# Three of the four branch products of the first two layers computed as split products, their weights parted in place by ScalarE and VectorE

## What is computed

```
gates = sigmoid(h @ w_in[:, gate columns])          # 256 x (4 * 1024)
merged = sum over b of gates[b] * (y[b] @ w_branch[b])   # y[b]: 256 x 256, w_branch[b]: 256 x 1024
x = x + merged @ w_out
```

## Time and profile before

| | |
|---|---|
| median of three runs | 2550.53 us (2550.09 to 2550.73) |
| the profiled execution, its own time | 2556.48 us |
| its span | 2554.7 us |
| PE busy, share of the span | 95% |
| DVE, ACT, POOL busy, share of the span | 67%, 54%, 16% |
| mean granted clock of PE | 0.972 |

### The profile page before, as it was taken

One profiled execution on the slowest core, in us unless ns is written; L12 is line 12 of the kernel. 1 busy time (PEld: TensorE's weight loads), 2 busy tenths in 40 slices (PEclk: granted clock), 3 DMA queues, 4 the chain that ended last, 5 costly groups with the idle time before them and its releaser, 6 DMA issues.

```text
span 2554.7 us, 31962 instructions
## 1 busy us (share of the span) xinstructions
PE 2414.3 (95%) x11845; PEld 1962.0 (77%) x11845; DVE 1708.3 (67%) x2332; ACT 1376.3 (54%) x1737; POOL 409.3 (16%) x225
## 2 busy tenths in 40 slices
PE   6999999899987999999999999899989989998998
PEld 6986788798766778778787787677768867776886
DVE  4848655566675889889889898863565555356554
ACT  4543344454422778778778787635334444533443
POOL 2155000003530000000000000065500006560000
PEclk9999999999997999999999999999999999999999
DMA  7434465244232999999999999653465525346550
GB/s 224 165 116 169 168 223 198 91 151 163 102 131 95 365 338 350 346 331 364 330 330 365 328 345 351 223 170 132 149 229 191 198 76 172 132 149 222 190 198 34
DMA packets 381700, 549.38 MB, mean 215 GB/s; under 512 B 27220, under 2 KB 283592, under 8 KB 381464
## 3 DMA queue, kind: packets, MB, share of 16 engines
q1 hardware_dynamic: 377392, 535.82, 61.5%
q0 software_dynamic: 3920, 11.58, 1.7%
q10 hardware_dynamic: 288, 0.59, 0.1%
HBM read 546.91 MB, written 1.05 MB: 214 GB/s over the span
## 4 chain that ended last, share of the span: by engine, by line
PE 83%; DVE 11%; DMA 3%; ACT 2%; issue 1%; POOL 0%; DVEq 0%; SPq 0%; ACTq 0%
PE mb L907 14%; PE mb L909 14%; PE mb L908 14%; PE pb L907 8%; PE pb L909 8%; PE pb L908 8%; DMA ring<-in_w_in 3%; PE pb L1356 2%; PE mb L1266 1%; PE pb L1027 1%; PE pb L1306 1%; DVE w_lo L2553 1%; PE pb L890 1%; PE mb L1054 1%; PE mb L1282 1%
## 5 line engine op out<-in xcount | busy, mean ns | idle before, releaser
L2553 DVE TENSOR_TENSOR w_lo<-ring,w_hi 128x1024 fp32r<-128x1024 f32 x444 | 533.5, 1222 | 193.4 <-ACT w_hi L1652 168.7
L1652 ACT ACTIVATE w_hi<-ring 128x1024 fp32r<-128x1024 f32 x340 | 348.2, 1054 | 310.9 <-PE pb L909 119.1
L907 PE MATMUL mb<-w_hi,hT_hi 128*128 128x512 f32 x1232 | 494.1, 401 | 3.0 <-DVE w_lo L2553 2.6
L909 PE MATMUL mb<-w_lo,hT_hi 128*128 128x512 f32 x1232 | 481.5, 391 | 0.0
L759 POOL TENSOR_TENSOR w_lo<-ring,w_hi 128x1024 fp32r<-128x1024 f32 x152 | 372.4, 2477 | 448.6 <-ACT w_hi L1652 448.5
L907 PE MATMUL pb<-w_hi,hT_hi 128*128 128x512 f32 (+1 forms) x928 | 355.7, 383 | 19.3 <-DVE low_rows L2553 6.8
L2553 DVE TENSOR_TENSOR w_lo<-down_w,w_hi 128x1024 fp32r<-128x1024 f32 x242 | 293.9, 1223 | 88.2 <-ACT w_hi L1652 79.5
L909 PE MATMUL pb<-w_lo,hT_hi 128*128 128x512 f32 (+1 forms) x928 | 346.3, 373 | 0.0
L908 PE MATMUL pb<-w_hi,low_rows 128*128 128x512 f32 (+1 forms) x928 | 346.3, 373 | 0.0
L1800 ACT ACTIVATE w_hi<-ring 128x1024 fp32r<-128x1024 f32 x256 | 267.3, 1057 | 17.7 <-PE mb L909 14.2
L908 PE MATMUL mb<-w_hi,xg_lo 128*128 128x512 f32 x704 | 275.3, 391 | 0.0
(11 more groups left out here) (461 smaller groups left out, 3742.9 us busy)
## 6 DMA issues: line engine op xcount, KB each, us to landing
ring<-in_moe_w SPq DMA_DIRECT2D x128, 1024.0 KB, 7.9
ring<-in_w_in SPq DMA_DIRECT2D x50, 2048.0 KB, 8.1
down_w<-in_moe_w SPq DMA_DIRECT2D x88, 1024.0 KB, 11.2
third_gu<-in_moe_w SPq DMA_DIRECT2D x48, 1024.0 KB, 9.5
down_w<-in_w_ffn_down SPq DMA_DIRECT2D x22, 1024.0 KB, 9.9
ring<-in_w_out SPq DMA_DIRECT2D x8, 2048.0 KB, 7.8
ring<-in_ffn_w SPq DMA_DIRECT2D x16, 1024.0 KB, 7.8
ring<-in_w_ffn_gate SPq DMA_DIRECT2D x16, 1024.0 KB, 5.4
```

The source lines that it names most:

```text
L907: mm(o, a_hi, hi, start=start, stop=False)
L909: return mm(o, a_hi, lo, start=False, stop=stop)
L1652: f(w_hi[:, m % NPIECE], src, ACT.Copy).then_inc(w_hi_ready, 1)
L2553: return tt(dst, src, hi.bitcast(F32), ALU.subtract)
```

## The change

`SPLIT_BRANCHES = (0, 1, 3)`: the branch products of b = 0, 1 and 3 become split products, in both layers; b = 2 stays plain.

* PE: the eight plain products of a `merge` become 24 matmuls on `fp32r` operands; for each bank four with the high part of the turned rows, then a wait for their low part, then two with it.
* ACT: before `yturned(L, b)` for b = 0 and 1, and before the gates (3, 1) for b = 3, a new `branch_high`: two copies of 128 x 1024 from `ring` to the high part (`ring_parts`, the free half of the same slot; for b = 3 `ch_parts`, which lies on `ch_in`).
* DVE: `branch_low` ahead of take_y(1), take_y(2) and take_y(3): two subtractions of 128 x 1024, written over the weights; each waits for ACT's copy. And `yT_low`: one subtraction of 128 x 512 out of the bank of the turned rows, between the reading of the next y and its head_norm for b = 0 and 1, ahead of merge(3) for b = 3.
* The bank of `yturn` is emptied by DVE (`yT_low`) for these branches, no longer by ACT.

```diff
+SPLIT_BRANCHES = (0, 1, 3)
@@ PE
             def merge(L, b, hs=range(2)):
+                if b in SPLIT_BRANCHES:
+                    _, w_high, w_low = (w.rearrange("p (k n) -> p k n", k=2) for w in branch_parts(L, b))
+                    pe.wait_ge(yT_hi_ready, nth_split(L, b))
+                    for h in hs:
+                        cols = slice(h * 512, (h + 1) * 512)
+                        for i in range(T):
+                            it = slice(i * P, (i + 1) * P)
+                            bank = open_bank(BK[L], ("merge", b, h, i))
+                            pe.wait_ge(branch_split, 2 * nth_split(L, b))
+                            for kk in range(2):
+                                mm(bank[:], yT_parts[:, 0, kk, it], w_high[:, kk, cols], start=kk == 0, stop=False)
+                                mm(bank[:], yT_parts[:, 0, kk, it], w_low[:, kk, cols], start=False, stop=False)
+                            acted(BK[L], ("yturn", b))
+                            for kk in range(2):
+                                ins = mm(bank[:], yT_parts[:, 1, kk, it], w_high[:, kk, cols], start=False, stop=kk == 1)
+                            ins.then_inc(filled, 1)
+                    return
@@ ACT
+            def branch_high(L, b):
+
+                s, landed = find[(L, "branch", b)]
+                act.wait_ge(arrived[s], landed)
+                if b == 3:
+                    act.wait_ge(gla_mm, 5 * L + 5)
+                w, hi, _ = branch_parts(L, b)
+                for kk in range(2):
+                    f(hi[:, kk * D:(kk + 1) * D], w[:, kk * D:(kk + 1) * D], ACT.Copy).then_inc(branch_hi_ready, 1)
...
-                high_to(M + 24)
+                branch_high(L, 0)
                 yturned(L, 0)
...
+                branch_high(L, 1)
                 yturned(L, 1)
...
                 high_to(M + 42)
+                branch_high(L, 3)
                 gate(L, 3, 1)
                 yturned(L, 3)
@@ DVE
+            def branch_low(L, b):
+
+                w, hi, lo = branch_parts(L, b)
+                for kk in range(2):
+                    n, cols = 2 * nth_split(L, b) - 1 + kk, slice(kk * D, (kk + 1) * D)
+                    v.wait_ge(branch_hi_ready, n)
+                    tt(lo[:, cols], w[:, cols], hi[:, cols].bitcast(F32), ALU.subtract).then_inc(branch_split, 1)
+
+            def yT_low(L, b):
+
+                B = BK[L]
+                v.wait_ge(yT_hi_ready, nth_split(L, b))
+                tt(yT_parts[:, 1].rearrange("p k s -> p (k s)"), pb[B.index[("yturn", b)] % 4][:],
+                   yT_parts[:, 0].rearrange("p k s -> p (k s)").bitcast(F32), ALU.subtract).then_inc(dve_emptied, 1)
...
+                branch_low(L, 0)
                 take_y(L, 1)
...
                 ins.then_inc(o_read, 1)
+                yT_low(L, 0)
                 v.wait_ge(o_read, 4 * L + 2)
                 head_norm(L, 1, 3, u_ml[:, :, ML_O:ML_O + MW], False)
                 merge(L, 0)
...
+                branch_low(L, 3)
                 take_y(L, 3)
...
                 low_range(M + 40, M + 42)
+                yT_low(L, 3)
                 merge(L, 3)
```

More of the change, by code:

```diff
@@ L238, in __init__ @@
         self.jobs = jobs
-        self.by = ["dve" if j[0] in ("merge", "wout") or (j[0] == "turn" and 4 <= j[1] < 8) else "act" for j in jobs]
+        self.by = ["dve" if j[0] in ("merge", "wout") or (j[0] == "turn" and 4 <= j[1] < 8)
+                   or (j[0] == "yturn" and len(j) == 2 and j[1] in SPLIT_BRANCHES) else "act" for j in jobs]
         n_act, n_dve = self.by.count("act"), self.by.count("dve")
@@ L276, in sem @@
             return ctx.enter_context(nc.semaphore(name))
+        with ExitStack() as split_memory:
+            ring_parts = split_memory.enter_context(nc.sbuf_tensor("ring_parts", [P, 2, SLOTW], F32R))
         ring = sb("ring", [P, 2, SLOTW])
@@ L313, in build @@
             u_ml = mix("u_ml", [P, T, ML_O + MW + 8])
+            with ExitStack() as split_memory:
+                ch_parts = split_memory.enter_context(nc.sbuf_tensor("ch_parts", [P, 8, S], F32R))
             ch_in = mix("ch_in", [P, 13, S])
@@ L318, in build @@
             y = mix("y", [P, T, MW])
+            with ExitStack() as split_memory:
+                yT_parts = split_memory.enter_context(nc.sbuf_tensor("yT_parts", [P, 2, 2, S], F32R))
             yT = mix("yT", [P, 2, 2, S])
@@ L453, in build @@
         e_hi_ready, e_split, e_used, xg_hi_ready = (sem(s) for s in ("e_hi_ready", "e_split", "e_used", "xg_hi_ready"))
+        branch_hi_ready, branch_split, yT_hi_ready = sem("branch_hi_ready"), sem("branch_split"), sem("yT_hi_ready")
         router_in, logits_mm, ex_arg, ex_ready = sem("router_in"), sem("logits_mm"), sem("ex_arg"), sem("ex_ready")
@@ L515, in build, with branch_parts, nth_split @@
                 used_at[m] = n_used
+        def branch_parts(L, b):
+            s, at = find[(L, "branch", b)][0], 2 * D * (b == 3)
+            hi = ch_parts[:].rearrange("p b s -> p (b s)") if b == 3 else ring_parts[:, s, 2 * D:4 * D]
+            return ring[:, s, at:at + 2 * D], hi, ring_parts[:, s, at:at + 2 * D]
+        def nth_split(L, b):
+            return 3 * L + SPLIT_BRANCHES.index(b) + 1
         def place_used(m):
@@ L1026, in merge @@
                         for kk in range(2):
-                            ins = mm(bank[:], yT[:, b % 2, kk, i * P:(i + 1) * P], w[:, kk, h * 512:(h + 1) * 512],
+                            ins = mm(bank[:], yT[:, 0, kk, i * P:(i + 1) * P], w[:, kk, h * 512:(h + 1) * 512],
                                      start=kk == 0, stop=kk == 1)
@@ L1684, in yturned @@
                 B = BK[L]
-                empty(B, job, (yT[:, b % 2].rearrange("p k s -> p (k s)"), pb[B.index[job] % 4][:], ACT.Copy, 1.0))
+                if b in SPLIT_BRANCHES:
+                    act.wait_ge(filled, B.filled(job))
+                    f(yT_parts[:, 0].rearrange("p k s -> p (k s)"), pb[B.index[job] % 4][:], ACT.Copy).then_inc(yT_hi_ready, 1)
+                else:
+                    empty(B, job, (yT[:, 0].rearrange("p k s -> p (k s)"), pb[B.index[job] % 4][:], ACT.Copy, 1.0))
+            def branch_high(L, b):
[6 more added lines that the diff above has]
+                    f(hi[:, kk * D:(kk + 1) * D], w[:, kk * D:(kk + 1) * D], ACT.Copy).then_inc(branch_hi_ready, 1)
             def mixers(L):
@@ L2297, in mixers @@
                 gla_factors(L, 1)
+                branch_low(L, 1)
                 take_y(L, 2)
@@ L2301, in mixers @@
                 ins.then_inc(o_read, 1)
+                yT_low(L, 1)
                 v.wait_ge(o_read, 4 * L + 3)
```

## The result

The changed kernel takes 2595.85 us (median of four runs, 2590.54 to 2598.03), against 2550.63 (2550.09 to 2553.6) for the kernel before: ratio 1.0172, 95% interval 1.0154 to 1.019. Slower, by 45 us; forecast were 2591.5, in 2568 to 2606. The profiled execution's own time is 2598.03, its span 2596.2, its mean granted clock 0.966.

The account below looks back on a forecast made before the run. PE, busy 95% of the span, was taken as the bound, meeting DVE at waits. Layer 0's +21.3 and layer 1's +19.7 make +41.0 on the median of 2550.53: 2591.5 us, range 2568 to 2606.

Parts of the forecast that it names:

- Branch 0: Layer 0: DVE's late norm meets POOL's batch, four Newton steps blocked; gate (2, 0) starts at 202.1, +7.6, +9.3 with clock.
- Branch 1: Layer 0: DVE's lateness and POOL's batch delay the bank for gate (3, 0): start +14.8, +15.1 after clock and round 1.
- the blocks: Ahead of gate (3, 0): all four POOL pieces block DVE before the bank, two more than before, 2.05 each, 4.1 us.
- The clock: After PE's gaps ahead of gates (2, 0) and (3, 0): slow clock loses 1.7 us each; 0.9 after branch 3's stall.
- Branch 3: DVE waits for ACT's late copies; PE stalls 5.9 us, merge(3) ends +5.3, and the clock adds 0.9.
- the 1.6 less that I took: Layer 1 already had a 3.95 us gap ahead of gate (3, 0), so it adds +19.7 against layer 0's +21.3.
- PE's saving: Merges of the six split branches: 24 matmuls take 5.45 us against 7.03, 1.6 less a branch, 9.5 in all.
- its other price of a merge: By the skill's four passes for true FP32, three of four take 5.27 us; the sum would be 1.1 us lower.
- that the work costs only its own time (2572): Rival: Newton steps slip between POOL's pieces, gate (2, 0) starts +2.5; +11 a layer, 2572; 14%.
- that the clock costs more (2605): Rival: six gaps of 6 to 9 us each lose twice as much, take_y(2) at 11.7; 13.6 more, 2605; 10%.
- that only branch 3 hurts (2561): Rival: POOL's batch is itself late enough to let the norm through; +5.3 a layer, +10.6, 2561; 4%.
- the faster one (2541): Rival: DVE's added work falls into its 9.03 us idle time ahead of 180.82, PE's 9.5 us are gained; 2541; 4%.

Follow-up runs that it names:

- the short pieces: GpSimd subtracts 16 of 1024 columns in the pieces of gates (2, 0) and (3, 0): changed kernel 1.0057, kernel before 0.9953.
- the held batch: Changed kernel, GpSimd waiting for y of branches 1 and 2 ahead of its batches for gates (2, 0) and (3, 0): 2578.6 us, ratio 1.0103.
- the first two single-branch runs: Against the kernel before, only branch 0 split: ratio 1.0051; only branch 1 split: ratio 1.0062.
- the early copies: Changed kernel, ACT's copies of branch 0 ahead of its wait for the scores, branch 3's ahead of two `w_out` pieces: 1.0041; with GpSimd also waiting for y, 1.0012.

## Why the prediction was right, and where its sizes were off

The direction and the mechanism held, step by step:

* **Branch 0.** Predicted were a start of gate (2, 0) at 202.1 after a stall of 8.9; measured 202.22 after 9.12. The four blocked instructions were there, but they were not the ones named. I had let three small instructions without a second SBUF operand pass and counted four Newton steps; three of the four blocked ones were just those (L2130, L2036, L2037). The count, one for each of POOL's pieces, gave the same end.
* **Branch 1.** Predicted +14.8 at the start of gate (3, 0), measured +17.15. The batch was at 232.41 (predicted 232.0) and hit four instructions, the last three 128x512 in the norm. The term that was mis-sized most is the blocks: 4.1 us was taken for two more of them, 5.7 came. Before, the two blocked additions alternate with multiplications of 0.69 us that read PSUM and go on beside the batch, and lose 1.3 us each:

```profile
224.16 2.02 DVE L2113 TENSOR_TENSOR merged<-merged,gates 128x512 f32<-128x512 f32 x1
...
226.94 2.00 DVE L2113 TENSOR_TENSOR merged<-merged,gates 128x512 f32<-128x512 f32 x1
```

In the norm four stand one behind the other and lose 2.0 to 2.2 each, 8.4 in all against 2.6. The prediction priced the two new ones and let the two old ones stand. The rest is DVE's lateness at take_y(2): 227.56 - 216.60 = 10.96, of which 10.0 had been taken; `yT_low` cost 0.5 instead of 0.7. PE's wait at GLA round 1 did vanish.

* **The clock.** I took 1.7 us a gap, from a place in the kernel before where PE had waited 4.30 us (the 3.95 of the prediction is the idle part of a window of 4 us). The windows above show 0.50 until about 208.2: PE's matmuls came 0.427 us apart for 6 us (202.79 to 203.21 for one), 14 of them, and each lost 0.2: 2.8 us. This is the other mis-sized term of the sum. Two such gaps a layer make 2.2 us; the first is part of the lateness at take_y(2).
* **Branch 3.** Predicted were a stall of 5.9 and transposes released by the norm; measured 5.93.
* **Sum.** At the end of layer 0's stage +24.3 (predicted 21.3), at the end of layer 1's +47.2 (41.0). Layer 1 added 22.9, 1.4 less than layer 0, close to the 1.6 less that I took; so both layers miss by the same 3 us. In layer 0 they are 1.6 for the blocks, 0.7 for the lateness at the norm of branch 2, 1.0 for the clock behind the second gap, less 0.3 at branch 3.
* **PE's saving.** The prediction says that the 9.5 us that PE saves are in its sum. No term holds them: both gates start when DVE has emptied a bank, and DVE sets the pace of merge(3). So its other price of a merge, 5.27 us, would not have moved the sum by 1.1 us either.

Between layer 1 and the end the profiled execution gave back 5.7 us (47.2 down to 41.5), which no step foresaw; by chance its span hit the predicted +41.0. Nearly all of it can be read at one place. In layer 2 ACT waits for a load of `in_w_in`, and PE for ACT's `u_ret` behind it. Before:

```profile
1687.88 2.00 ACT L1652 ACTIVATE w_hi<-ring 128x1024 fp32r<-128x1024 f32 x2 [12.55 <-DMA ring<-in_w_in]
1691.00 0.66 PE L1410 MATMUL mb<-cst,u_ret 128*64 128x128 f32 x2 [4.13 <-ACT u_ret L1589]
...
1706.78 0.60 PE L1419 MATMUL mb<-cst,u_ret 128*128 128x128 f32 x4
```

After:

```profile
1732.19 2.01 ACT L1688 ACTIVATE w_hi<-ring 128x1024 fp32r<-128x1024 f32 x2 [8.63 <-DMA ring<-in_w_in]
1735.31 0.41 PE L1446 MATMUL mb<-cst,u_ret 128*64 128x128 f32 x2 [1.39 <-ACT u_ret L1625]
...
1748.63 0.60 PE L1455 MATMUL mb<-cst,u_ret 128*128 128x128 f32 x4
```

The wait is 2.7 us shorter. And the work behind it, up to L1419 or L1455, takes 13.3 us instead of 15.8: before, the granted clock is 0.50 in the 4 us behind the wait, after it is 1.00. The lateness is 41.85 us there. In the twelve experiments the same wait of PE is between 1.2 and 6.4 us; why the load lands earlier in some of them was not tried. The medians, +45.2 us, lie between the stages' 47.2 and the span's 41.5. So the closeness of 2591.5 to the measured 2595.85 is luck in part: the stages cost 6.2 us more than forecast, and a place that the forecast did not look at gave some of it back.

**Shares.** By the stages of both layers (46.8 us): the meeting with GpSimd 23 (by the short pieces; 16 by the held batch, which brings waits of its own), branch 3's late copies 14. The rest, some 10, is DVE's added work of 3.1 us a branch and the clock behind what gaps remain, less what PE saves; these were not parted further.

The rivals: that the work costs only its own time (2572) falls with the blocked rows; that the clock costs more (2605) had the right sign and about a third of its size (1.1 us more at each of four gaps, 4.4 of 13.6); that only branch 3 hurts (2561) is refuted by the first two single-branch runs; the faster one (2541) needed the early copies, and with them and the held batches three branches come to 2554.

## What to carry to other kernels

Before adding work to DVE, look at what GpSimd starts in the microseconds after it: a delay of 2.6 to 4 us became a gap of 9 to 12, because a chain of short instructions slid under a batch of four long ones. A chain that just misses such a batch is a hazard also for changes that make another engine faster. Price a gap on PE with the slow microseconds behind it, and put copies for a later product ahead of the waits that they don't need.

## What the runs showed of the hardware

* Beside GpSimd's batches DVE got one instruction on SBUF operands through for each GpSimd instruction, however small: 128x8 took 1.92 to 2.42 us instead of 0.17, 128x512 2.71 to 2.91 instead of 0.69. TENSOR_SCALAR with a single SBUF operand, float32 and int32, was held up like the rest (1.92, 2.29 and 2.27). The Trainium skill, "SBUF — State Buffer", section Who interferes with whom, says that `tensor_scalar` can enter modes of DVE that use both ports, when its operands meet conditions, and can contend with GpSimd in them. This trace agrees so far as these three were held up; in which mode they ran, no run shows. The prediction had applied only the same section's rule on two SBUF inputs.
* In the held kernel DVE's multiplications with one operand in PSUM stayed at 0.69 us beside a batch (228.67, 231.70 and 234.45), while the additions between them, on SBUF alone, took 2.28, 1.99 and 2.01.
* GpSimd pieces of 128x16 (0.22 to 0.25 us) held nothing up: DVE's 128x8 stayed at 0.17.
* Behind gaps of 9.1 and 10.1 us PE ran its first matmuls at a granted clock of 0.50, 0.427 us apart instead of 0.227. After a gap of 2.76 in the held kernel before the first matmul took 0.47 us, after 4.58 it took 0.77 or 0.65, after 5.20 it took 0.77.
